# Attention values moved to the head of the step in three mixers of a four-layer hybrid backbone

## The reference

```python
s = einsum(q, k) * scale          # A: window mask, D: window and bias added
p = softmax(concat([s_latent, s_cached, (sink)]))
o = einsum(p, v)                  # then merge_heads(o) @ w_o, gated, added to x
```

## Time and profile before

| | us |
|---|---|
| median of 3 runs | 2916.22 (2915.5 to 2918.16) |
| the profiled execution | 2915.18 |
| its span, first to last instruction | 2913.2 |
| TensorE busy | 2887.1 (99%) |
| VectorE busy | 2275.1 (78%) |
| ScalarE busy | 1253.1 (43%) |

### The profile page before, as it was taken

How to read it: one execution, slowest core, us unless ns; L and a number is a source line. 1 busy time by engine, 2 the same in 40 slices (tenths; PEclk the granted TensorE clock), 3 DMA queues, 4 the chain that set the end, 5 groups by cost and what they waited for, 6 DMA issues and landing times.

```text
span 2913.2 us, 44421 instructions
## 1 busy us (share of the span) xinstructions
PE 2887.1 (99%) x17591; PEld 2805.3 (96%) x17591; DVE 2275.1 (78%) x3461; ACT 1253.1 (43%) x2010; POOL 161.1 (6%) x171
## 2 busy tenths in 40 slices
PE   8999999999999999999999999999999999999999
PEld 6999979999999998999999998899999999989999
DVE  6999987888788887888888877778888887777653
ACT  4332564443333366443333348644333334664432
POOL 0000210000000030000000012100000001310000
PEclk9999999999999999999999999999999999999999
DMA  7556314455455512555555531254554555324342
GB/s 297 211 213 234 125 44 179 183 194 215 178 190 201 205 69 96 186 183 211 192 183 196 205 115 56 83 195 183 202 203 182 191 216 189 109 75 179 124 148 91
DMA packets 87866, 490.22 MB, mean 168 GB/s; under 512 B 11840, under 2 KB 13184, under 8 KB 51648
## 3 DMA queue, kind: packets, MB, share of 16 engines
q1 hardware_dynamic: 83840, 480.42, 44.4%
q0 software_dynamic: 3904, 8.24, 1.1%
HBM read 485.33 MB, written 3.29 MB: 168 GB/s over the span
## 4 chain that ended last, share of the span: by engine, by line
PE 57%; issue 38%; DVE 2%; ACT 1%; DMA 1%; POOL 0%; POOLq 0%; DVEq 0%; ACTq 0%
PE ps L866 16%; PE ps L885 8%; PE ps L871 8%; PE ps L918 5%; PE ps L1113 4%; PE ps L889 4%; PE ps L850 1%; PE ps L1048 1%; PE ps L1197 1%; PE ps L1088 1%; DMA boot<-in_mod_w 1%; PE ps L1033 1%; PE ps L1029 1%; PE ps L955 0%; PE ps L1133 0%
## 5 line engine op out<-in xcount | busy, mean ns | idle before, releaser
L866 PE MATMUL ps<-h_hi,w_hi 128*128 128x386 f32 x2688 | 908.1, 338 | 0.0
L866 PE MATMUL ps<-h_lo,w_hi 128*128 128x386 f32 x2688 | 893.2, 332 | 0.0
L1714 DVE TENSOR_TENSOR w_lo<-w_raw,w_hi 128x2048 fp32r<-128x2048 f32 (+4 forms) x280 | 701.1, 2504 | 26.7 <-ACT w_hi L1358 26.4
L1741 DVE CUSTOM_DVE_ANT_0 F_junk<-F_slab,cond,mod_b 128x1024 f32<-128x1024 f32 x544 | 707.1, 1300 | 12.9
L1358 ACT ACTIVATE w_hi<-w_raw 128x2048 fp32r<-128x2048 f32 (+3 forms) x273 | 566.4, 2075 | 11.0 <-DMA w_raw<-in_ffn_dn 9.2
L866 PEld LDWEIGHTS ps<-h_lo,w_hi 128*128 128x128 f32 x2688 | 512.5, 191 | 0.0
L866 PEld LDWEIGHTS ps<-h_hi,w_hi 128*128 128x128 f32 x2688 | 503.0, 187 | 0.0
L871 PE MATMUL ps<-h_hi,w_lo 128*128 128x386 f32 x2688 | 494.2, 335 | 0.0
L885 PE MATMUL ps<-F_act_hi,w_hi 128*128 128x384 f32 x1408 | 473.6, 336 | 0.0
L885 PE MATMUL ps<-F_act_lo,w_hi 128*128 128x384 f32 x1408 | 473.3, 336 | 0.0
L871 PEld LDWEIGHTS ps<-h_hi,w_lo 128*128 128x128 f32 x2688 | 468.8, 187 | 0.0
(11 more groups left out here) (407 smaller groups left out, 3502.7 us busy)
## 6 DMA issues: line engine op xcount, KB each, us to landing
w_raw<-in_ffn_gu SPq DMA_DIRECT2D x175, 1024.0 KB, 4.8
F_slab<-in_mod_w SPq DMA_DIRECT2D x272, 512.0 KB, 5.6
w_raw<-in_ffn_dn SPq DMA_DIRECT2D x64, 1408.0 KB, 6.4
w_raw<-in_d_w SPq DMA_DIRECT2D x8, 1536.0 KB, 6.7
boot<-in_mod_w SPq DMA_DIRECT2D x8, 1024.0 KB, 7.8
w_raw<-in_a_w SPq DMA_DIRECT2D x4, 1536.0 KB, 6.6
w_raw<-in_b_w SPq DMA_DIRECT2D x4, 1536.0 KB, 6.3
w_raw<-in_c_w SPq DMA_DIRECT2D x8, 544.0 KB, 3.7
```

The lines of the kernel that those rows point to most:

```text
L866: pe.matmul(ps[:, 2 * par + u, 0:N_MOVE], w[0][:, k, u, :], h[:, k, :], start=(k == 0 and h is h_hi), stop=False)
L1714: dve.tensor_tensor(w_lo[par][:, 0:w], w_raw[par][:, 0:w], w_hi[par][:, 0:w], ALU.subtract).then_inc(w_split_lo.sem, 1)
L1741: dve.tensor_tensor_reduce(out=junk[:], in0=w, in1=cond[:, c, :], scale=scale, scalar=mod_b[:, n:n + 1], op0=ALU.mult, op1=ALU.add, accum_ ...
```

## The change

In the steps that have filling projections, in A, B and D and from step 3 on, TensorE does `values(b - 3)` ahead of `scores(b)`. In the even ones of them, ScalarE does `o_hi` as the first thing of the step.

```diff
                 for b in range(BATCHES + 3):
                     first, last = ahead(kind, b)
+                    beside = kind != "C" and b >= 3 and bool(fills(kind, b))
+                    if beside:
+                        values(s, b - 3, "cl")
                     if b < BATCHES:
                         scores(s, b)
...
                     else:
-                        if b >= 3:
+                        if b >= 3 and not beside:
                             values(s, b - 3, "cl")
                         if turn:
                             turn_qk(s, (b + 1) // 2, "qk")
...
                 for b in range(BATCHES + 3):
...
+                    out_pair = b >= 4 and b % 2 == 0
+                    beside = kind != "C" and bool(fills(kind, b))
+                    if out_pair and beside:
+                        o_hi(s, b // 2 - 2)
                     if 2 <= b < BATCHES + 2 and not (per_pair(kind) == 1 and b == BATCHES - 3):
                         p_copy(s, b - 2)
-                    if b >= 4 and b % 2 == 0 and not fills(kind, b):
+                    if out_pair and not fills(kind, b):
                         o_hi(s, b // 2 - 2)
...
-                    if b >= 4 and b % 2 == 0 and fills(kind, b):
+                    if out_pair and fills(kind, b) and not beside:
                         o_hi(s, b // 2 - 2)
```

## The result

| | before | after |
|---|---|---|
| median of 6 runs each, us | 2915.86 (2914.85 to 2918.16) | 2927.27 (2927.01 to 2929.01) |
| the profiled execution | 2915.18 | 2928.6 |
| its span | 2913.2 | 2926.6 |
| TensorE busy | 2887.1 | 2889.1 |

A forecast was written before the change was run, and what follows sets the result against it. The prediction took TensorE's instruction stream to bound the filling steps. Its terms summed to +13.0 us, which on the median of 2916.22 gave 2929.2 us, range 2922.0 to 2933.0, or 2927.9 to 2930.4 for its own case alone.

The forecast's parts named there:

- (a): Nine odd steps of A, B, D: turn_qk waits bare for ScalarE's copies of p, +0.85 us each, +7.65 us.
- (b): Six even steps with two projections through bank 7: the second waits for raw of the first, +0.74 us each, +4.44.
- (c): Step 5 of A and B: the next projection tile waits for the raw copy, +0.43 us each, +0.86 us.
- (d): Step 4 of A and B: neither handoff, only the saved array switch, 2 x -0.17 = -0.34 us.
- (e): D's step 3: the first values wait for the raw copy that empties bank 6, +0.73 us.
- (g): A's step 8: an output matmul's wait for VectorE's weight split goes, -0.34 us; later waits for scaled p unchanged.
- (f): Even batches' values at the step's head need o_lo earlier; o_hi moved for that; taken as 0, at most +0.56 us.
- 1 (the switches alone): Filling steps of A, B, D: only saved array switches count, no added waits; -3.6 us, 2912.6; chance 0.06.
- 2 (p's handoff alone): Filling steps: the handoff of p costs time, that of raw doesn't; +6.3 us, 2922.6; chance 0.08.
- 4 (many values waiting for o_lo): Filling steps: values at the front wait for o_lo, nine times 0.6 us, +5.4 us, 2934.6; chance 0.06.
- 3: Faster: VectorE's lead removes later waits for A's p and D's o_lo; 8.1 us less, 2908.1; chance 0.04.
- Rival 5: TensorE's new waits in the filling steps drop its clock to 1.2 GHz: ten us more, 2939; chance 0.03.

The follow-up runs named there:

- turn_first: The kernel before the change, with turn_qk ahead of values in the nine odd steps, values still behind the scores: 2926.12 us, ratio 1.0032.
- cover_p: The changed kernel, with six projection matmuls between the transposes of p and turn_qk in the nine odd steps: 2921.41 us, ratio 1.0016 to before.
- o_hi_back: The changed kernel, with ScalarE's o_hi back at its old place behind the exponentials: 2933.23 us, ratio 1.0061 to the kernel before.
- odd_d_only: The kernel before the change, with values ahead of the scores in D's odd filling steps alone: 2921.39 us, ratio 1.0017.
- both_covers: The changed kernel with projection matmuls before turn_qk, p's transposes between paired projections, some steps left as before: 2914.42 us, ratio 0.9993 to before.

## Why the forecast held, step by step

| term | forecast | measured in the timelines |
|---|---|---|
| (a) nine odd steps | +7.65 | +7.36 |
| (b) six even steps, raw | +4.44 | +3.93 |
| (c) step 5 of A, B | +0.86 | +0.72 |
| (d) step 4 of A, B | -0.34 | -0.31 |
| (e) D's first values | +0.73 | +0.74 |
| (g) A's tail | -0.34 | -0.15 |
| sum | +13.0 | +12.3 |

(a) Right. Six of the nine steps cost 0.82 to 0.85 us. In the three that are the first of their mixer to wait (step 3) it is 0.78: turn_qk came 1.60 us behind the transposes, not 1.66. turn_first and cover_p show from two sides that it is the cover.

(b), (c) Right in kind, mis-sized in one term, the handoff from `raw` to the next projection. I had taken 0.14 us from p's copy; it is 0.05: the copy in the rows above ends at 2519.43 + 0.49 = 2519.92, the projection starts at 2519.97. Eight places at 0.09 less are 0.7 us; the two terms came out 0.65 us lower, nearly the whole difference of the sums. The range allowed 0 to 0.21.

(d) Right: -0.19 us in B and -0.12 in A. The 0.07 us missing in A is o_lo: in A's step 4 the projections took 3.42 us instead of 3.35 before the values of step 5 could start, the place that (f) had named as close. VectorE's row shows where it ended, 368.32 us, and the values started at 368.46:

```profile
367.77 0.55 DVE L2114 TENSOR_TENSOR A_oT_lo<-ps,A_oT_hi 128x384 fp32r<-128x384 f32 x1
```

(e) Right: 0.67 us of wait in the row L1085 <- D_raw, and the values start 0.74 us after the point where the scores would have (2502.99 to 2503.73). The copy that they wait for ends at 2503.09 + 0.49 = 2503.58:

```profile
2503.09 0.49 ACT L1452 ACTIVATE D_raw<-ps 128x384 f32<-128x384 f32 x1
...
2503.73 0.44 PE L1085 MATMUL ps<-D_pt,D_raw 128*64 128x128 f32 x4 [0.67 <-ACT D_raw L1452]
```

(f) Nearly right at 0 for the change as made: the 0.07 us under (d) are all of it. But the text had the time to spare from D's rows alone. In A and B the move of o_hi is what keeps the values from 5.2 us of waiting (o_hi_back). In D the 3.84 us that VectorE stood for o_hi are gone, as forecast.

(g) Half right. The 0.34 us in step 8 is gone, but TensorE now waits more for VectorE's scaled p: L1048 <- A_p counts five instead of four times, 3.8 us instead of 3.3. The first of these waits, in step 9:

```profile
394.35 0.87 PE L1048 MATMUL ps<-ident,A_p 128*128 128x128 f32 x6 [0.39 <-DVE A_p L2106]
```

In step 9 this is still made up, since turn_qk's wait for the copy of p falls from 0.49 to 0.22 us: from the scores of step 8 to those of step 10 it is 8.00 us instead of 8.39. In step 10 the transposes come late as well (their weight load stands 0.31 us for the scaled p), and at the scores of step 11 only 0.18 us of the lead is left (11.69 instead of 11.87). The tail of A hangs on VectorE, so most of what TensorE saves there is given back within three steps.

Of the rivals, 1 (the switches alone) and 2 (p's handoff alone) fall with the waits above; 4 (many values waiting for o_lo) does not happen in the change, but cover_p and o_hi_back come upon it; 3 fell with (g), the waits for A's p grew instead of vanishing. Rival 5 fell too: TensorE stood for 0.79 and 0.58 us once each in every 20.7 us of D, and the granted clock was 1.00 in the three stretches, the 2.4 GHz level. The section on HAM oscillation in the Trainium skill, "TensorE: Matmul & The Clock Gate", tells of a clock that falls during waits for DMA between bursts of matmuls. Those waits are longer than these, so the three stretches neither bear it out nor speak against it. The drain that "TensorEngine Tiling (Array Packing)", Key Properties, states fits the 0.17 us that a switch costs in the rows, and by that rule alone the change would have gained 3.2 us.

The level was forecast 1.9 us too high, and the measured 2927.27 lies 0.6 us under the band of 2927.9 to 2930.4 that the forecast gave for its own case, though inside the wide range. The sum itself, 12.3, is inside its bounds of 11.7 to 14.2. Of the 1.9 us 0.7 is the sum and 0.36 the median of before, which three more runs moved from 2916.22 to 2915.86. The rest fits how many executions of each kernel had the slow stretch described below: the forecast added the sum to a median 1.04 us above the profiled execution, but four of the six executions of after were at 1.000.

## What to carry to other kernels

Before a group of matmuls is moved, ask what stood on both sides of it: if its neighbours share a PSUM bank and another engine must empty it in between, the group was their cover, and the move costs copy plus handoff minus what is left. Here, with the saved switch of 0.17 us already taken off, a step with a bare handoff lost 0.65 to 0.85 us, and step 5 of A and B, where part of the cover stayed, 0.36. Work without a dependence on that bank (here six projection matmuls, 1.15 us) can take over as cover; then see which buffer's release is next in line.

## What the runs showed of the hardware that I had not expected

- The gap from the end of an engine's copy to TensorE's start is not one number. From ScalarE it is 0.05 us to a projection matmul (2519.92 to 2519.97), 0.15 us to the values (D's step 3: 2503.58 to 2503.73) and to turn_qk's transposes (2507.06 to 2507.21). From VectorE's o_lo to the values it is 0.14 us as well (383.21 to 383.35 in o_hi_back), but from VectorE's normed q to turn_qk's transposes 0.06 (382.29 to 382.35 in turn_first). So the kind of matmul that starts doesn't settle it alone, and why some starts are quicker stays open.
- The profiled execution of after has a short stretch at a lower granted clock in the first FFN, at 33 to 37 us. The window of 34 to 38 us of after, and then of before:

```profile
34.00:38.00 4.00, 4.00 (x17) 3.98 (x16) 3.87 (x10) 4.00 (x11) 0.00 (x0) 0.64 0.30 119
```

```profile
34.00:38.00 4.00, 4.00 (x24) 3.81 (x23) 3.87 (x10) 4.00 (x11) 0.00 (x0) 1.00 0.30 119
```

TensorE does 17 instead of 24 matmuls there. In the timeline of after the pairs start 0.65 us apart:

```profile
35.55 0.85 PE L1254 MATMUL ps<-h_hi,w_lo 128*128 128x386 f32 x2
36.20 0.83 PE L1257 MATMUL ps<-h_lo,w_hi 128*128 128x386 f32 x2
```

and in that of before, where the clock was full, 0.36:

```profile
36.04 0.52 PE L1254 MATMUL ps<-h_hi,w_lo 128*128 128x386 f32 x2
36.40 0.52 PE L1257 MATMUL ps<-h_lo,w_hi 128*128 128x386 f32 x2
```

From 34 to 36 us the granted clock is 0.50, the 1.2 GHz level. The first six groups of matmuls behind the wait for h_hi take 3.71 us in after (33.13 to 36.84) and 2.39 us in before (33.30 to 35.69): 1.3 us dearer. Ahead of it TensorE had stood for 0.72 us for ScalarE's h_hi, but before stood there for the same 0.72 us at full clock. In odd_d_only such a stretch came at 1765 to 1770 us instead (0.66), also 1.3 us dearer, and in both_covers at 1764 to 1768 us (0.62), in each behind a wait of 1.68 us; before stood there for 1.69 us at full clock. These three are the profiled executions at 0.999; the five at 1.000 hold no such stretch. Of the six executions of after the four with a mean clock of 1.000 took 2927.01 to 2927.35 us, the two with 0.999 took 2928.6 and 2929.01. Of the 42 executions of before that were measured beside the experiments, the eleven at 1.000 took up to 2914.92 us and the 31 at 0.999 took 2916.34 to 2919.00. So most of the scatter of one kernel's runs goes with such stretches; what sets one off stays open.
